# Recurrence of a hybrid layer: the transposed 32x32 inverse from VectorE block transposes instead of a third TensorE product per level

## The chip, the cores and the metric

One core of a Trainium2 chip runs the whole layer as one program. The metric is the device time of that program in microseconds (us), as the median of several executions. A profile is one execution of its own, with its own time.

## The reference

The layer takes x (1024 tokens by 1024 channels, float32) through an adaLN-modulated hybrid time mixer, a layer norm, a squared-ReLU MLP and a second layer norm. The part that matters here is the first branch of the mixer, an RWKV-7 recurrence with 8 heads of 64 channels:

```
def step(state, inp):
    r_t, w_t, k_t, v_t, a_t, b_t = inp
    sa = jnp.einsum('bhvk,bhk->bhv', state, a_t)
    state = (state * w_t[:, :, None, :] + sa[..., None] * b_t[:, :, None, :]
             + v_t[..., None] * k_t[:, :, None, :])
    return state, jnp.einsum('bhvk,bhk->bhv', state, r_t)
```

The other branch (stick-breaking attention), the merge by gates, the output projection and the MLP are not touched.

## The kernel before

The program is a row of stages: `phase_start` (adaLN, input projection), `phase_recurrence` (L809), `phase_stick`, `phase_merge`, `phase_out`, `phase_mlp`. Only `phase_recurrence` and a table of constants are changed. In the profile that stage's repeated part runs from 260 us to about 630 us.

The recurrence is computed in chunks of 64 tokens. A turn handles 2 heads (one half of the partitions each) and half of the tokens, which is 8 chunks, so there are 8 turns for 4 pairs of heads and 2 halves. Within a chunk the step by step update becomes a triangular solve: with N the strictly triangular 64x64 matrix of products between writes and reads, the kernel needs T = (1 - N)^-1. It builds T for the 32x32 diagonal blocks (8 blocks in the free direction times 4 quadrants of partitions, so 32 blocks at a time), starting with the 2x2 blocks and doubling the size four times: at each level T grows by T (level mask of N) T. The last step, from 32 to 64, is done apart with the products L1589 and L1597.

Both T (`Ts`) and its transpose (`TTs`) are kept, since TensorE takes one operand transposed. One level k = 0 to 3 before the change is:

- `correction` on TensorE (L1487): X = N T, 32 small products, which the profile shows as 64 matmul records of 32x32 since float32 products run as two records each. They write the bank `rw_invx`.
- `correction` on VectorE (L1232): takes X out of PSUM and multiplies it by the mask of the level.
- `corrected` on TensorE: T X into `rw_invx` (L1495, 64 records) and its transpose into `rw_inv` (L1498, 64 records), which accumulates over the levels.
- `inverse` on VectorE (L1228): adds the new part to `Ts`. `inverse` on ScalarE (L953): copies `rw_inv` to `TTs`.

Before level 0, `tt0` (mask times N, L1245, plus the identity, L1247) is put into both banks by products with the identity (L1530: 8 records, L1533: 64 records), and copied from there (L1224, L953).

Each engine's order is written out by hand in its own `turn(t)`; the engines meet by semaphores (`wait`), and a waiting instruction holds up all that is behind it on its engine. Five things are interleaved in a turn: the inverse for turn t; the front (decays, keys, norms) of turn n = t+1; the chain of 8 states of turn l = t-1 (L1380 on TensorE, L1169 on VectorE, each needing the other); the group norm of turns ll = t-2 (L1401, L1430) and lll = t-3 (L1360 spread, L1199 `normalised`, L1205 `gained`, L1212 `added`, L1423 `gate`). So group-norm work exists only from turn 3 on. On VectorE, `cumulate` (L1096) starts the front of the next turn, and then POOL runs L878, L882, L885, L887, L891. The reads of keys (L1236) take a whole 128x512 result out of PSUM with a mask.

PSUM has 8 banks, all taken: `BA`, `BB` (`rw_main`), `BC` (`rw_inv`), `BD` (`rw_invx`), `F` (`rw_front`), `TL` (`rw_tail`), `HY0`, `HY1` (`rw_state`). The logits of the decay (L1340) and of the rate (L1346) both go through `F`, one after the other.

Of the kernel before, what the change touches and what calls it, by code (L numbers as in the profile page):

```python
# [9 lines left out]
ALU = mybir.AluOpType  # L10
# [3 lines left out]
P = 128  # L14
# [31 lines left out]
CT = {n: i for i, n in enumerate(("ident", "causal", "small", "small2", "bones", "cent", "ahead", "misc"))}  # L46


def constants():
# [6 lines left out]
    lower = lambda s: (row // (2 * s) == col // (2 * s)) & (row % (2 * s) >= s) & (col % (2 * s) < s)  # L56
    t[:, CT["small"]] = np.select([which == 0, which == 1, which == 2, which == 3],
                                  [(row // 2 == col // 2) & (row < col), lower(2), lower(4), lower(8)])
    t[:, CT["small2"]] = np.select([which == 0, which == 1], [lower(16), row == col], 0)
# [8 lines left out]
    t[:, CT["misc"], 5] = i[:, 0] % CH < CH // 2  # L68
    reset = np.ones((P, HALF), np.float32)
# [739 lines left out]
def phase_recurrence(nc, g, a):  # L809

    with ExitStack() as es:
# [16 lines left out]
        NTs, tt0 = sb("NTs", (P, NB, 2 * B)), sb("tt0", (P, NB, B))  # L828
# [6 lines left out]
        per_turn = {"pp": 2, "M1e": 2, "NTe": 2, "M2e": 2, "ze": 2, "ge": 2, "ysb": 2, "PQ": 2, "TTe": 5, "Te": 5, "X": 4, "Xe": 4, "TX": 4,  # L835
                    "ch": NC, "S": NC}
        names = ("wa gs th kkr sq lw sg la a cum cumE eN eE eI t k2 aN ss ssm rn bc w1 AT RT BT KT wc rk BhT KhT M0 pp TT0 M1e NTe init TTe Te "
# [74 lines left out]
        def _(act):  # L912
# [19 lines left out]
            def learning_rate(n):  # L932
                if not inside(n):
                    return
                wait(act, n - 1, "k2")
                wait(act, n - 1, "aN")
                wait(act, n, "la")
                act.activation(av[:], F[:], ACT.Sigmoid, bias=col(n, A0)).then_inc(s["a"], 1)
# [20 lines left out]
            def state_maps(l):  # L959
                if not inside(l):  # L960
                    return
                wait(act, l, "ZG")
                for c2 in (1, 0):
                    if c2 == 0:
                        wait(act, l, "ze", 1)
                    act.activation(gt[:, c2::2, :], q4(BCD[c2])[:, :, HD:P], ACT.Copy).then_inc(s["ge"], 1)
# [39 lines left out]
            def turn(t):  # L1006
                f, n, l, ll, lll = t % 2, t + 1, t - 1, t - 2, t - 3
                wait(act, t, "M0")
                for e in (1, 0):
                    if e == 0:  # L1010
                        wait(act, t, "pp", 1)
                    act.activation(flat(NTs[:, 4 * e:4 * e + 4, :]), BAB[e][:, 0:2 * P], ACT.Copy).then_inc(s["NTe"], 1)
                state_maps(l)
                deviation(lll)
                inverse(t, 0)
                decay_rate(n)
                keys(n)
                inverse(t, 1)
                learning_rate(n)
                inverse(t, 2)  # L1020
                decays(n)
                inverse(t, 3)
                natural(t, "vn", flat(vn[:]), BA[:])
                natural(t, "kn", flat(kn[:]), BB[:])
                high(lll)
                inverse(t, 4)
                wait(act, t, "TTe")
                act.activation(T64[:, :, 0:B], TTs[:], ACT.Copy, scale=g.misc(5)).then_inc(s["TTm"], 1)
                natural(t, "bn", W[f][:, :, 1, :].rearrange("p (e j) n -> p j e n", e=2), q4(BA).rearrange("p j (e n) -> p j e n", e=2))
                natural(t, "an", rhs[:, :, 0:HD].rearrange("p (e j) n -> p j e n", e=2), q4(BB).rearrange("p j (e n) -> p j e n", e=2))  # L1030
                centred(ll)
                wait(act, t, "T12")
                act.activation(T64[:, :, B:CH], BC[:, 0:2 * P].rearrange("p (b n) -> p b n", n=B), ACT.Copy).then_inc(s["T12e"], 1)
                wait(act, t, "mv")
                act.activation(rhs[:, :, HD:P], BA[:].rearrange("p (b n) -> p b n", n=HD), ACT.Copy).then_inc(s["mve"], 1)
                squared(ll)
                answers(l)
# [44 lines left out]
        def _(dve):  # L1082
            small = lambda x: g.tile("small")[:, x * B:(x + 1) * B]
            over = lambda m, k: m.unsqueeze(1).to_broadcast([P, k, m.shape[-1]])
            sum32 = lambda x: g.tile("small2")[:, x * B:(x + 1) * B]
            m16, eye = sum32(0), sum32(1)
            levels = (small(1), small(2), small(3), m16)
# [84 lines left out]
            def queries(l):  # L1172
# [3 lines left out]
                for c2 in range(2):  # L1176
                    if c2:
                        wait(dve, l, "ge", 1)
                    dve.tensor_tensor(c8(zt)[:, c2::2, :], q4(BCD[c2])[:, :, 0:HD], ar[l % 2][:, 1, :].rearrange("p (c n) -> p c n", n=CH)[:, c2::2, :],
                                      ALU.add).then_inc(s["ze"], 1)  # L1180
# [40 lines left out]
            def inverse(t, k):  # L1221
                if k == 0:
                    wait(dve, t, "init")
                    dve.tensor_copy(flat(Ts[:]), BD[:, 2 * P:4 * P]).then_inc(s["Te"], 1)  # L1224
                else:
                    wait(dve, t, "TX", k)
                    wait(dve, t, "Te", k)
                    dve.tensor_tensor(flat(Ts[:]), BD[:, 2 * P:4 * P], flat(Ts[:]), ALU.add).then_inc(s["Te"], 1)  # L1228

            def correction(t, k):  # L1230
                wait(dve, t, "X", k + 1)
                dve.tensor_tensor(X[:], BD[:, 0:2 * P].rearrange("p (b n) -> p b n", n=B), over(levels[k], NB), ALU.mult).then_inc(s["Xe"], 1)  # L1232
# [6 lines left out]
            def turn(t):  # L1239
                f, n, l, ll, lll = t % 2, t + 1, t - 1, t - 2, t - 3  # L1240
                wait(dve, t, "M0")
                for e in range(2):
                    if e:
                        wait(dve, t, "NTe", 1)
                    dve.tensor_tensor(tt0[:, 4 * e:4 * e + 4, :], half4(BAB[e], 0)[:, :, 0:B], over(small(0), NT), ALU.mult).then_inc(s["pp"], 1)  # L1245
                wait(dve, t, "pp")
                dve.tensor_tensor(tt0[:], tt0[:], over(eye, NB), ALU.add).then_inc(s["TT0"], 1)  # L1247
                queries(l)
# [6 lines left out]
                write_hats(t)  # L1255
                correction(t, 0)
                reads_of_keys(t, 0)
                reads_of_keys(t, 1)
                inverse(t, 1)
                state(l, 0)  # L1260
                key_hats(t)
                correction(t, 1)
                state(l, 1)
                cumulate(n)
                inverse(t, 2)
                state(l, 2)
                normalised(lll)
                correction(t, 2)
                state(l, 3)
                gained(lll)  # L1270
                added(lll)
                inverse(t, 3)
                state(l, 4)
                gated(lll)
                correction(t, 3)
                state(l, 5)
                keys(n)
                inverse(t, 4)
# [6 lines left out]
                writes(n)  # L1285
                ends(n)
# [13 lines left out]
            queries(end)  # L1300
# [26 lines left out]
        def _(pe):  # L1327
            ident, bones = g.tile("ident"), g.tile("bones")
            eye = lambda rows: g.tile("small2")[rows, B:2 * B]
# [5 lines left out]
            def decay_logits(n):  # L1335
# [3 lines left out]
                wait(pe, n - 1, "AT")  # L1339
                pe.matmul(F[:], wa_s[0:LORA_W, n // 2 * P:(n // 2 + 1) * P], th[0:LORA_W, tok(n)], start=True, stop=True).then_inc(s["lw"], 1)  # L1340

            def rate_logits(n):
                if not inside(n):
                    return
                wait(pe, n, "sg")
                pe.matmul(F[:], wa_s[LORA_W:P, n // 2 * P:(n // 2 + 1) * P], th[LORA_W:P, tok(n)], start=True, stop=True).then_inc(s["la"], 1)  # L1346
# [967 lines left out]
```

## Time and profile before

| what | value |
| --- | --- |
| median of 3 executions | 2004.65 us (2004.02 to 2005.7) |
| the profiled execution | 2001.76 us, its span 2000.0 us |
| PE matmul busy | 1767.2 us (88%), 18163 records |
| PE weight load busy | 946.4 us, 18298 |
| DVE (VectorE) busy | 778.6 us, 1057 |
| ACT (ScalarE) busy | 569.0 us, 871 |
| POOL busy | 460.2 us, 241 |

The engines are named as in the profile: PE is TensorE (PEld its weight loads), DVE is VectorE, ACT is ScalarE. A duration of a matmul record contains its way through the array, and neighbours overlap, so the time that a group of products takes is read from the start of the group to the start of the next. Idle time with the releaser "issue" is time in which an engine waited for nothing that the profile shows. The granted clock of TensorE has two levels, written 1.00 (2.4 GHz) and 0.50 (1.2 GHz), and a number in between is a mean over a stretch.

### The profile page before, as it was taken

The page shows a single profiled execution, that of the slowest core. Times are in us where ns is not written, and L with a number is a line of the kernel's source. Part 1 is how long each engine was busy: PE and PEld are TensorE (multiplying, and loading weights), DVE is VectorE, ACT ScalarE, POOL GpSimd, SP SyncE. Part 2 cuts the span into 40 slices and gives each one's busy share as a digit, 9 for nine tenths or more (in the row PEclk, how much of TensorE's full clock was granted, in tenths as well). Part 3 has the DMA queues.
Part 4 walks back from the last instruction along what each step waited for, and adds up shares of the span by engine and source line. Part 5 has one row for each costly group of instructions (what it writes and reads, how often), then busy time and mean ns, then how long its engine had stood idle before and what let it go on. Part 6 is the DMA issues. An engine that isn't in the chain of part 4 may idle for free. (4 is left out here: it accounts for less than half of the span.)

```text
span 2000.0 us, 41125 instructions
## 1 busy us (share of the span) xinstructions
PE 1767.2 (88%) x18163; PEld 946.4 (47%) x18298; DVE 778.6 (39%) x1057; ACT 569.0 (28%) x871; POOL 460.2 (23%) x241
## 2 busy tenths in 40 slices
PE   2699778888878999988999978779999999999995
PEld 2344356666665445554444434334444444444442
DVE  7766443344442145561010148732312223122238
ACT  4111133343322135561211134433131221312202
POOL 1221021111112101111222221335251322513213
PEclk7799967787988999999999989889999999999998
DMA  9334100000010112001212221022111211212002
GB/s 332 116 126 136 52 3 4 4 4 4 4 47 23 36 50 54 1 1 43 63 34 60 105 85 32 21 95 85 53 56 40 72 31 52 67 37 85 1 1 84
DMA packets 105491, 109.93 MB, mean 55 GB/s; under 512 B 2428, under 2 KB 82442, under 8 KB 105098
## 3 DMA queue, kind: packets, MB, share of 16 engines
q1 hardware_dynamic: 105352, 107.82, 16.6%
q8 instruction: 119, 1.95, 0.4%
q14 instruction: 20, 0.16, 0.0%
HBM read 101.52 MB, written 4.19 MB: 53 GB/s over the span
## 5 line engine op out<-in xcount | busy, mean ns | idle before, releaser
L207 PE MATMUL tokens_ps<-a_hi,z 128*128 128x512 bf16 x944 | 246.9, 380 | 6.9 <-POOL z L2032 6.1
L520 PE MATMUL ff_ps<-ff_hi,c_lo 128*128 128x512 bf16 x504 | 191.0, 379 | 0.6
L520 PE MATMUL ff_ps<-ff_hi,c_hi 128*128 128x512 bf16 x500 | 189.5, 379 | 1.3 <-DVE z L2210 0.9
L520 PE MATMUL ff_ps<-ff_lo,c_hi 128*128 128x512 bf16 x500 | 189.5, 379 | 0.6
L2210 DVE TENSOR_TENSOR z<-ff_ps,z 128x512 f32<-128x512 f32 x128 | 88.3, 690 | 205.7 <-PE ff_ps L520 205.0
L2103 ACT ACTIVATE ff_r<-tokens_ps,cols 128x1024 f32<-128x1024 f32 x32 | 35.6, 1112 | 418.9 <-PE tokens_ps L207 409.2
L2032 POOL TENSOR_TENSOR z<-z 128x1024 bf16<-128x1024 f32 x30 | 70.1, 2335 | 363.7 <-ACT z L2028 363.7
L207 PEld LDWEIGHTS tokens_ps<-a_hi,z 128*128 128x128 bf16 x960 | 94.2, 98 | 120.7 <-POOL z L2032 7.1
L207 PE MATMUL tokens_ps<-a_lo,z 128*128 128x512 bf16 x469 | 141.1, 380 | 0.6
L2196 DVE TENSOR_TENSOR ff_r<-ff_r 128x1024 f32<-128x1024 f32 x32 | 44.8, 1401 | 230.1 <-ACT ff_r L2103 230.1
L1739 DVE TENSOR_TENSOR mg_ga<-mg_ga,mg_ps 128x1024 f32<-128x1024 f32 x8 | 9.8, 1221 | 202.9 <-PE mg_ps L207 202.9
L184 POOL TENSOR_TENSOR mg_wlo<-mg_stage,mg_whi 128x1024 bf16<-128x1024 f32 x21 | 44.7, 2128 | 172.1 <-ACT mg_whi L180 172.1
L207 PE MATMUL mg_ps<-a_hi,mg_whi 128*128 128x512 bf16 x248 | 75.5, 384 | 6.1 <-POOLq L78 5.7
L520 PEld LDWEIGHTS ff_ps<-ff_hi,c_hi 128*128 128x128 bf16 x512 | 50.1, 98 | 61.6 <-issue 1.3
L520 PEld LDWEIGHTS ff_ps<-ff_hi,c_lo 128*128 128x128 bf16 x512 | 50.1, 98 | 60.5
L520 PEld LDWEIGHTS ff_ps<-ff_lo,c_hi 128*128 128x128 bf16 x512 | 50.1, 98 | 60.3
L207 PE MATMUL mg_ps<-a_hi,mg_wlo 128*128 128x512 bf16 x256 | 77.1, 383 | 0.0
L2142 POOL TENSOR_TENSOR c_lo<-ff_r,c_hi 128x1024 bf16<-128x1024 f32 x32 | 68.0, 2125 | 36.7 <-ACT c_hi L2107 36.7
L207 PE MATMUL mg_ps<-a_lo,mg_whi 128*128 128x512 bf16 x248 | 75.3, 383 | 0.4
L650 DVE TENSOR_TENSOR_SCAN b_lo<-z,sb_ahead 128x256 f32<-128x256 f32 (+3 forms) x32 | 55.9, 1788 | 49.2 <-ACT z L751 49.2
L207 PEld LDWEIGHTS tokens_ps<-a_lo,z 128*128 128x128 bf16 x480 | 47.1, 98 | 56.9 <-issue 0.6
L207 PE MATMUL zs_ps<-a_hi,zs_whi 128*128 128x512 bf16 x210 | 64.3, 383 | 9.0 <-POOL zs_wlo L184 8.1
(333 smaller groups left out, 3282.0 us busy)
## 6 DMA issues: line engine op xcount, KB each, us to landing
ada_w<-w_ada SPq DMA_DIRECT2D x9, 2048.0 KB, 7.9
z<-w_ff SPq DMA_DIRECT2D x32, 512.0 KB, 4.0
ff_st<-w_ff SPq DMA_DIRECT2D x8, 2048.0 KB, 7.7
mg_stage<-w_in SPq DMA_DIRECT2D x16, 512.0 KB, 3.8
zs_stage<-w_in SPq DMA_DIRECT2D x14, 512.0 KB, 5.2
z<-w_ada SPq DMA_DIRECT2D x3, 2048.0 KB, 15.8
z<-w_in SPq DMA_DIRECT2D x8, 512.0 KB, 4.5
z<-w_out SPq DMA_DIRECT2D x1, 4096.0 KB, 14.9
```

Of the source, the lines that this page charges most:

```text
L184: pool.tensor_tensor(lo[u][:], stage[u][:], hi[u][:], ALU.subtract).then_inc(lo_ready[u], 1)
L207: last = pe.matmul(out[:, h * HALF:(h + 1) * HALF], w[:, kt, :], a[:, slot, h * HALF:(h + 1) * HALF], start=(x == 0 and y == 0), stop=(x = ...
L520: last = pe.matmul(out, a[:, slot, at], w[:, x, n], start=(x == 0 and y == 0), stop=(x == k - 1 and y == 2))
L650: dve.tensor_tensor_scan(prod[b][:, 0:nk][:, ::-1], m, masked, 1.0, ALU.mult, ALU.max).then_inc(s_scan, 1)
L1739: dve.tensor_tensor(ga[:], ga[:], ps[2][:], ALU.mult).then_inc(s_pa, 1)
L2032: pool.tensor_tensor(ff.lo[u], stage[u], ff.hi[u], ALU.subtract).then_inc(ff.lo_ready[u], 1)
L2103: act.activation(r[u][:], ps1[u][:], ACT.Relu, bias=g.cols[:, ds(gr * GT + (b1 + t), 1)]).then_inc(s_relu[u], 1)
L2142: pool.tensor_tensor(g.c_lo[:, GT * par + t, :], r[u][:], g.c_hi[:, GT * par + t, :], ALU.subtract).then_inc(s_ulo[u], 1)
L2196: dve.tensor_tensor(r[u][:], r[u][:], r[u][:], ALU.mult).then_inc(s_sq[u], 1)
L2210: dve.tensor_tensor(acc, ps2[x % 4][:], acc, ALU.add).then_inc(s_acc, 1)
```

## The change

The third product per level and the products with the identity go. `Ts` and `TTs` are related by a VectorE transpose of 32x32 blocks: `TTs` is now the first one built (mask times N plus identity) and `Ts` is its transpose; after each level, `Ts` gets its addition and is transposed into `TTs`. The four level masks are applied once per turn, to N (`NTm`, two VectorE instructions of 128x512 out), so the copy of X needs no mask and moves to ScalarE. The last level's lower part of `T64` is written by three instructions instead of one. Since the bank `rw_inv` is free during the levels, the rate logits go there and both logits products are issued together, behind `correction(t, 0)`. The orders on all engines are rearranged: `normalised` goes ahead of the second `inverse`, `gained` and `added` go between `cumulate` and `state(l, 3)`, `high` goes behind `squared`.

```
-                  [(row // 2 == col // 2) & (row < col), lower(2), lower(4), lower(8)])
-    t[:, CT["small2"]] = np.select([which == 0, which == 1], [lower(16), row == col], 0)
+    upper = lambda s: (row // (2 * s) == col // (2 * s)) & (row % (2 * s) < s) & (col % (2 * s) >= s)
+    t[:, CT["small"]] = np.select([which == 0, which == 1], [upper(1), row == col], 0)
+    t[:, CT["levels"]] = np.select([which == k for k in range(4)], [upper(2 << k) for k in range(4)])
...
 ScalarE
-            def inverse(t, k):
-                wait(act, t, *(("TX", k) if k else ("init",)))
-                act.activation(flat(TTs[:]), BC[:, 0:2 * P], ACT.Copy).then_inc(s["TTe"], 1)
+            def correction(t, k):
+                wait(act, t, "X", k + 1)
+                act.activation(flat(X[:]), BD[:, 0:2 * P], ACT.Copy).then_inc(s["Xe"], 1)
...
 VectorE
             def inverse(t, k):
...
+                wait(dve, t, "TX", k + 1)
+                wait(dve, t, "Te", k + 1)
+                dve.tensor_tensor(flat(Ts[:]), BD[:, 2 * P:4 * P], flat(Ts[:]), ALU.add).then_inc(s["Te"], 1)
+                wait(dve, t, "Te", k + 2)
+                dve.transpose(flat(TTs[:]), flat(Ts[:])).then_inc(s["TTe"], 1)
...
+                dve.tensor_tensor(TTs[:], TTs[:], over(eye, NB), ALU.add).then_inc(s["TT0"], 1)
+                wait(dve, t, "TT0")
+                dve.transpose(flat(Ts[:]), flat(TTs[:])).then_inc(s["Te"], 1)
+                queries(l, 1)
                 wait(dve, t, "NTe")
+                for e in range(2):
+                    dve.tensor_tensor(NTm[:, 4 * e:4 * e + 4, :, :], half4(BAB[e], 0)[:, :, 0:B].unsqueeze(2).to_broadcast([P, NT, 4, B]), levels,
+                                      ALU.mult).then_inc(s["NTm"], 1)
+                queries(l, 0)
...
+                write_hats(t)
                 inverse(t, 0)
                 reads_of_keys(t, 0)
                 reads_of_keys(t, 1)
                 state(l, 0)
                 key_hats(t)
                 state(l, 1)
+                normalised(lll)
+                inverse(t, 1)
+                state(l, 2)
                 cumulate(n)
                 gained(lll)
                 added(lll)
+                state(l, 3)
+                inverse(t, 2)
+                gated(lll)
+                state(l, 4)
+                keys(n)
+                state(l, 5)
                 inverse(t, 3)
...
 TensorE
             def corrected(t, k):
-                wait(pe, t, "TTe", k + 1)
                 wait(pe, t, "Xe", k + 1)
+                if k:
+                    wait(pe, t, "TTe", k)
                 for e, j, b in blocks:
                     for q in quads:
-                        pe.matmul(BD[q, (NB + b) * B:(NB + b + 1) * B], TTs[q, b, :], X[q, b, :], start=True, stop=True)
-                for e, j, b in blocks:
-                    for q in quads:
-                        last = pe.matmul(BC[q, b * B:(b + 1) * B], X[q, b, :], TTs[q, b, :], start=False, stop=True, skip_group_check=True)
+                        last = pe.matmul(BD[q, (NB + b) * B:(NB + b + 1) * B], TTs[q, b, :], X[q, b, :], start=True, stop=True)
                 last.then_inc(s["TX"], 1)
...
-                for q in quads:
-                    pe.matmul(BC[q, 0:2 * P], eye(q), flat(tt0[q, :, :]), start=True, stop=True)
-                for e, j, b in blocks:
-                    for q in quads:
-                        last = pe.matmul(BD[q, (NB + b) * B:(NB + b + 1) * B], tt0[q, b, :], eye(q), start=True, stop=True)
-                last.then_inc(s["init"], 1)
                 answer_terms(l)
...
                 correction(t, 0)
+                logits(n)
+
+                corrected(t, 0)
...
                 chain(l, 0)
+
+                correction(t, 1)
                 deviations(lll)
                 chain(l, 1)
                 corrected(t, 1)
                 wait(pe, t, "M2e")
                 natural(t, "vn", zs(8, t), BA)
+                chain(l, 2)
+
+                correction(t, 2)
+                gate(lll)
+                chain(l, 3)
+
+                corrected(t, 2)
                 wait(pe, t, "KhT")
                 natural(t, "kn", kh, BB)
                 chain(l, 4)
+
+                correction(t, 3)
```

## Rows read from the trace of the kernel before

**Rows 1.** Stretches of one turn each (from:to, length, busy and instructions by engine, clock, DMA share, GB/s).

```profile
260.30:301.30 41.00, 31.59 (x1140) 25.63 (x1140) 13.67 (x29) 13.72 (x24) 6.25 (x5) 0.66 0.02 4
301.30:343.70 42.40, 36.24 (x1364) 30.08 (x1364) 16.40 (x40) 15.15 (x28) 6.25 (x5) 0.76 0.02 4
343.70:389.00 45.30, 39.91 (x1376) 31.30 (x1376) 16.96 (x41) 16.03 (x30) 6.26 (x5) 0.77 0.02 4
389.00:436.50 47.50, 41.44 (x1399) 31.63 (x1399) 20.04 (x46) 18.20 (x33) 7.35 (x6) 0.82 0.02 4
436.50:486.60 50.10, 43.52 (x1398) 33.77 (x1397) 21.14 (x46) 18.39 (x33) 7.55 (x6) 0.76 0.02 4
486.60:530.50 43.90, 37.38 (x1395) 29.07 (x1394) 20.93 (x46) 18.11 (x33) 7.55 (x6) 0.92 0.02 4
530.50:575.00 44.50, 36.32 (x1399) 28.14 (x1398) 20.95 (x46) 18.00 (x33) 7.54 (x6) 0.96 0.12 43
575.00:630.00 55.00, 39.44 (x1527) 32.33 (x1526) 16.01 (x41) 16.32 (x35) 8.95 (x9) 0.84 0.03 11
```

**Rows 2.** Order of time on PE in the turn from 486.6 us, single groups.

```profile
490.79 0.63 PE L1530 MATMUL rw_inv<-rec_tt,const 32*32 32x256 f32 x8
...
491.90 0.58 PE L1466 MATMUL rw_state<-c_lo,rec_vn 64*64 64x64 f32 x24
...
505.75 0.71 PE L1498 MATMUL rw_inv<-rec_TT,rec_X 32*32 32x32 f32 x62
506.38 0.33 PE L1380 MATMUL rw_state<-rec_st,rec_gt 64*64 64x64 f32 x4
507.86 1.10 PE L1423 MATMUL rw_tail<-z,rec_g_s 128*128 128x512 f32 x2 [1.14 <-DVE rec_yc L1199]
508.88 0.75 PE L1487 MATMUL rw_invx<-rec_T,rec_NTs 32*32 32x32 f32 x64
...
510.32 0.60 PE L1478 MATMUL rw_main<-const,rec_kh 128*128 128x128 f32 x4
```

**Rows 3.** Groups by line, 260 to 630 us (count, busy us, mean ns, idle before).

```profile
L1498 PE MATMUL rw_inv<-rec_TT,rec_X 32*32 32x32 f32 x2048 | 30.9, 206 | 16.1 <-issue 15.8
L1487 PE MATMUL rw_invx<-rec_T,rec_NTs 32*32 32x32 f32 x2048 | 30.3, 211 | 11.9 <-issue 9.8 <-DVE rec_T L1228 1.8
...
L1466 PE MATMUL rw_state<-c_lo,rec_vn 64*64 64x64 f32 x256 | 7.0, 226 | 7.0 <-issue 7.0
...
L1423 PE MATMUL rw_tail<-z,rec_g_s 128*128 128x512 f32 x10 | 6.4, 728 | 5.7 <-DVE rec_yc L1199 5.7
...
L1224 DVE COPY rec_T<-rw_invx 128x256 f32<-128x256 f32 x8 | 3.4, 424 | 7.0 <-PE rw_invx L1533 6.7
```

**Rows 4.** DMA queues, 486.6 to 530.5 us (packets, MB, share of the 16 engines).

```profile
q8 instruction: 11, 0.18, 1.7%
```

**Rows 5.** Order of time on DVE in the turn from 486.6 us, single instructions.

```profile
499.23 1.29 DVE L1236 TENSOR_TENSOR c_lo<-rw_main,const 128x512 f32<-128x512 f32 x2 [2.05 <-PE rw_main L1547]
...
504.50 1.22 DVE L1096 TENSOR_TENSOR_SCAN rec_cum<-reset,rec_sg 128x512 f32<-128x512 f32 x1
...
510.02 0.27 DVE L1169 SCALAR_TENSOR_TENSOR rec_st<-rec_st,rec_wc,rw_state 128x64 f32<-128x64 f32 x1
510.21 1.48 DVE L1205 TENSOR_SCALAR rec_yc<-rec_yc,cols 128x512 f32<-128x512 f32 x1
511.73 1.64 DVE L1212 TENSOR_TENSOR rec_yc<-rec_yc,rec_rk 128x512 f32<-128x512 f32 x1
...
517.04 0.54 DVE L1103 TENSOR_SCALAR rec_k<-rec_av,cols 128x512 f32<-128x512 f32 x1
```

**Rows 6.** Order of time on POOL in the same turn.

```profile
510.13 1.27 POOL L885 TENSOR_TENSOR rec_sg<-rec_kkr,rec_sg 128x512 f32<-128x512 f32 x1
511.36 1.45 POOL L887 TENSOR_TENSOR rec_ar<-z,rec_cum 128x512 f32<-128x512 f32 x1
```

**Rows 7.** A stretch with a long "issue" gap on PE (columns as in the first group).

```profile
466.50:467.80 1.30, 0.04 (x5) 0.00 (x0) 0.00 (x0) 0.21 (x1) 0.00 (x0) 1.00 0.00 0
...
468.90:482.40 13.50, 12.88 (x272) 9.63 (x272) 4.59 (x12) 4.15 (x8) 2.37 (x2) 0.50 0.02 4
```

More of the change, by code:

```diff
@@ L43 @@
 PAIR_ROWS = ("w0", "a0", "kk", "ka", "rk", "gng", "gnb")
-CT = {n: i for i, n in enumerate(("ident", "causal", "small", "small2", "bones", "cent", "ahead", "misc"))}
+CT = {n: i for i, n in enumerate(("ident", "causal", "small", "levels", "bones", "cent", "ahead", "misc"))}
 def constants():
@@ L962, in state_maps @@
                 wait(act, l, "ZG")
-                for c2 in (1, 0):
-                    if c2 == 0:
+                for c2 in range(2):
+                    if c2:
                         wait(act, l, "ze", 1)
@@ L1036, in turn @@
                 squared(ll)
+                high(lll)
                 answers(l)
@@ L1084, in _ @@
             over = lambda m, k: m.unsqueeze(1).to_broadcast([P, k, m.shape[-1]])
-            sum32 = lambda x: g.tile("small2")[:, x * B:(x + 1) * B]
-            m16, eye = sum32(0), sum32(1)
-            levels = (small(1), small(2), small(3), m16)
+            eye = small(1)
+            levels = g.const[:, CT["levels"], :].rearrange("p (k n) -> p k n", n=B).unsqueeze(1).to_broadcast([P, NT, 4, B])
             strict, incl = (g.tile("causal")[:, x * CH:(x + 1) * CH] for x in range(2))
@@ L1175, in queries @@
                 wait(dve, l, "ZG")
[L1176 to L1180, printed above, removed]
+                if c2 == 0:
+                    wait(dve, l, "ge", 1)
+                dve.tensor_tensor(c8(zt)[:, c2::2, :], q4(BCD[c2])[:, :, 0:HD], ar[l % 2][:, 1, :].rearrange("p (c n) -> p c n", n=CH)[:, c2::2, :],
+                                  ALU.add).then_inc(s["ze"], 1)
             def bonus(l):
@@ L1241, in turn @@
                 wait(dve, t, "M0")
+                wait(dve, l, "TTm")
                 for e in range(2):
@@ L1285, in turn @@
                 writes(n)
+                wait(dve, t, "T12")
+                wait(dve, t, "TTm")
+                dve.tensor_copy(T64[CH:CH + B, :, B:CH], BC[CH:CH + B, 0:2 * P].rearrange("p (b n) -> p b n", n=B)).then_inc(s["T12e"], 1)
                 ends(n)
@@ L1299, in _ @@
             end = TURNS - 1
-            queries(end)
+            queries(end, 1)
+            queries(end, 0)
             state0(end)
@@ L1333, in _, with logits @@
             blocks = [(e, j, 4 * e + j) for j in range(NT) for e in range(2)]
-            def decay_logits(n):
+            def logits(n):
                 if not inside(n):
@@ L1339, in decay_logits @@
                 wait(pe, n - 1, "AT")
+                wait(pe, n - 2, "ze")
+                wait(pe, n - 2, "ge")
                 pe.matmul(F[:], wa_s[0:LORA_W, n // 2 * P:(n // 2 + 1) * P], th[0:LORA_W, tok(n)], start=True, stop=True).then_inc(s["lw"], 1)
[L1342 to L1346, printed above, removed]
+                pe.matmul(BC[:], wa_s[LORA_W:P, n // 2 * P:(n // 2 + 1) * P], th[LORA_W:P, tok(n)], start=True, stop=True).then_inc(s["la"], 1)
             def squares(n):
@@ L1351, in squares @@
                 wait(pe, n, "sq")
-                wait(pe, n, "a")
+                wait(pe, n, "sg")
                 for j in range(NT):
@@ L1582, in turn @@
                 natural(t, "bn", bh, BA)
+                chain(l, 5)
+                corrected(t, 3)
+                bonus(ll)
                 wait(pe, t, "kne")
                 natural(t, "an", ar[f][:, 0, :], BB)
+                chain(l, 6)
                 wait(pe, t, "Te")
@@ L1588, in turn @@
                     for q in (0, 2):
-                        last = pe.matmul(BD[quads[q + 1], b * B:(b + 1) * B], NTs[quads[q], b, B:2 * B], Ts[quads[q], b, :], start=True, stop=True)
+                        last = pe.matmul(BD[quads[q + 1], b * B:(b + 1) * B], NTx[quads[q], b, :], Ts[quads[q], b, :], start=True, stop=True)
                 last.then_inc(s["X21"], 1)
@@ L1594, in turn @@
                 wait(pe, t, "TTe")
+                if inside(n):
+                    wait(pe, n, "a")
                 for e, j, b in blocks:
@@ L1618, in _ @@
             pe.wait_ge(s["th"], 2)
-            decay_logits(0)
-            rate_logits(0)
+            logits(0)
             squares(0)
```

95 lines of the change are left out of this document (25 added, 70 removed).

## The prediction, as put on record before the changed kernel was run

> **What bounds the kernel now.** Only the recurrence stage is touched, so I read that stage alone, first in stretches of one turn [rows 1]. A turn takes 41.0 to 50.1 us (the last stretch also holds the start of the tail). PE has products in flight for 31.6 to 43.5 us of it, DVE for 14 to 21, ACT for 14 to 18, POOL for 6 to 9. Such a busy share proves little, so the second view is the order of time on PE in one turn [rows 2]: group follows group, each starting a fraction of a microsecond after the one before, and the only real wait on another engine in a full turn is the one ahead of the gate product (1.14 us, until L1199 on DVE is done; 5.7 us over the 5 turns that have it [rows 3]). The dependence T, X, T X, T is hidden, since the order puts a chain step, a spread or a projection between each product and the next that needs it. PE's own instruction stream is the bound.
>
> The third view, the groups by line [rows 3], adds what the stream suffers from: idle time ended by "issue", 15.8 us ahead of records of L1498, 9.8 ahead of L1487, 7.0 ahead of L1466. The DMA queues say what this is [rows 4]: 11 packets of instructions, 0.18 MB, in one turn, so 16 KB each. A turn has 1395 matmul and 1394 weight-load records [rows 1]; 2789 over 11 is about 254 instructions a packet. PE runs dry where small records are issued faster than packets arrive.
>
> **The removed products.** L1498: 2048 records, 30.9 us busy in 32 groups [rows 3]; the last record of a group (about 0.19 us, nearly its mean of 206 ns) overlaps the next group, so 30.9 - 32 x 0.19 = 24.8 us of stream, mixed over both clocks (at the full clock a group takes 506.38 - 505.75 = 0.63 us [rows 2]). The products with the identity run from 490.79 to 491.90 [rows 2]: 1.11 x 8 = 8.9 us. Together **33.7 us**.
>
> What such a record costs is where a rule and the trace part. The row gives 0.63 us for 62 records, 10 ns each, since four quadrants run beside one another. The Trainium skill, TensorEngine Tiling (Array Packing), section Instruction Overhead, says that each matmul carries about 60 cycles of overhead however short it is; at 2.4 GHz that is 25 ns, and the 328 records removed per turn would be 8.2 us a turn, an estimate of 66 us in all. I take the row; the same page lets tiles overlap, and the trace shows it.
>
> **The "issue" gaps.** The bound above is that all 15.8 us ahead of L1498 go; the bound below is that they only move to the next dense group. A turn sheds 328 of 1395 records, 24%, and so 24% of the packets. 24% of 15.8 + 9.8 + 7.0 is 7.7 us. The neighbours that now meet (L1487 with a projection, L1495 with transposes) are less dense than L1495 with L1498. I take **10 us**, and keep 0 and 16.
>
> **The wait at the gate.** `normalised` moves ahead of the second `inverse`, and the gate product behind the third `correction`. The 5.7 us [rows 3] go: **5.7 us**.
>
> **What DVE gets.** Five transposes of 128x256 a turn, which the trace doesn't show. Nearest is the copy of the same shape, L1224, 0.42 us [rows 3]; below that I put nothing, above it a stretched instruction: L1205 took 1.48 us while POOL ran L885 and L887 [rows 5, 6], and the same form took 0.54 us with POOL idle (L1103 [rows 5]), a factor of 2.7, so 0.42 to 1.1 us. I take 0.42, 2.1 us a turn. The two `NTm` instructions read PSUM and write 128x512 each as the two of L1236 do: 1.29 us [rows 5]. One small copy for `T64` adds 0.4. What goes: four masked copies of X and the first copy of T, 5 x 0.42 = 2.1 us (ACT takes the copies of X in place of its own of `TTs`). Net +1.7 us on an engine busy 21 of 44 us: free, unless it falls on a step that PE waits for. There are two such steps.
>
> First, the head of a turn. `correction(t, 0)` needs `NTm`. From the end of M0, DVE does two masks (0.7), the identity (0.4), a transpose (0.4), one query (0.4) and `NTm` (1.3), 3.2 us by the prices above. PE has queries, state terms and answer terms in between, about 2.9 us without the 2 us of gaps that mostly fall there. I charge 0.2 us a turn: **-1.5 us**, and keep 0 to 8.
>
> Second, the middle. Between the second `inverse` and `state(l, 3)` DVE now has a transpose 0.42, a state 0.27, `cumulate` 1.22, `gained` 1.48, `added` 1.64 and the state 0.27 [rows 5]: 5.3 us. PE has in that time `correction` 0.63, the gate 508.88 - 507.86 = 1.02, a chain step 0.3, `corrected` 0.6 (as many small records) and a transposed tile 0.5 (its 0.60 less the overlap) [rows 2], 3.0 us, and then stands at chain(4), with `correction(t, 3)` behind it. So 2.3 us of new wait in the 5 turns with group norm: **-11.5 us**. It would be near 0 if POOL's work fell elsewhere, and 20 if transposes stretch too.
>
> **What I cost at nothing.** The paired logits are the same two products; their sigmoids come one after the other on ACT. The X copies on ACT (I price them as L1224, 0.42 us) are covered by the projection, spread, gate or squares that follow each `correction`; uncovered, each would show about 0.5 us, 32 times. The only one near its cover is the fourth, behind the exponentials of `decays`. The extra copies into `T64` end before PQ, behind two product groups and the norm spread (3 us). `high` moves to ACT's slack near the turn's end; POOL's low part follows in time for the next turn. No DMA is added, and SP's queue is untouched.
>
> **Sum.** 33.7 + 10 + 5.7 - 11.5 - 1.5 = 36.4 us. The profiled execution took 2001.76 us and would become 1965.4; the median of the runs lies 2.9 above it, so 1968.3, and I say **1968 us**.
>
> **Rivals.**
> 1. *The gaps go with L1498 and the middle wait is hidden* by them: 33.7 + 15.8 + 5.7 - 2 = 53 us, 1952. For it: the gaps are the larger part of what separates a turn from its bare stream. Against it: the head's dense part stays.
> 2. *DVE becomes the bound in the middle*: transposes at 1.1 us in the window in which POOL works, two to three of them per turn on the path, 2 us x 8 = 16 less: 1984. For it: the stretched L1205 and L1212. Against it: a transpose has one source, and only L1212, with two, and L1205 are seen stretched.
> 3. *The clock falls, and the result is slower.* PE stood still from 466.5 to 467.8 us at clock 1.00 and was then granted 0.50 for 13.5 us [rows 7]. With fewer records and a new wait of 2.3 us in the middle, such stretches could spread. The price: two turns with the same work took 50.1 us at 0.76 and 43.9 at 0.92 [rows 1], 0.39 us per 0.01 of mean clock. The mean over the turns is now 0.81; if all ran at the first turn's 0.66, that is 15 x 0.39 x 8 = 47 us lost against 36 won: 2015. It decides from a mean of 0.81 - 4.55/0.39/100 = 0.69 down. Against it: the long "issue" gaps, which are what stands ahead of the fall in the row, get fewer too. The Trainium skill, TensorE: Matmul & The Clock Gate, section HAM oscillation, warns of bursts with pauses between, and speaks against this change; by that rule the trace agrees, since the fall follows a pause.
> 4. *The stream was not what the turn's length came from*, and the shorter stream only waits elsewhere: within 4 us of 2004.65. Against it: a single wait on another engine in a full turn.
>
> **Chances.** Forecast (1956 to 1980) 0.62; rival 1 0.13; rival 2 (1980 to 2000) 0.13; rival 4 0.04; rival 3 0.08. The range takes in the forecast, most of rivals 1 and 2, and the bounds of the gaps (10 less, 6 more) and of the new waits (8 more, 9 less): 1946 to 1990. A measurement of this kernel tells 0.2%, 4 us, from no change. Faster 0.88, same 0.04, slower 0.08.
>
> **What would show it.** Right: a full turn has about 1067 matmul records and some 8 instruction packets; turns of 38 to 44 us; the first `state` after `added` ends a PE wait of about 2 us in turns 3 to 7; no wait ahead of the gate; transposes near 0.42 us; mean clock 0.76 to 0.86. The stages before and after unchanged. Wrong: PE waiting for `Xe` or `TTe` at several levels (the dependence is exposed after all), transposes of 1 us or more, a clock under 0.7, or turns shortened by less than 3 us with gaps merely moved to L1487 and L1495.

## The result, and the profile after

The median went from 2005.18 us (the kernel before, run again beside it) to 1916.34 us (1915.55 to 1919.04), a ratio of 0.955 with an interval of 0.952 to 0.958: 84 to 96 us less, where 36 had been forecast and 1946 was the lower end of the range. The direction was right, the size was not. The profiled execution has a span of 1914.1 us.

All of it lies in the recurrence. The first product of the value projection behind the turns (L1654, now L1638) starts at 546.4 us instead of 633.5, and the stages after it keep their lengths. The stretches of one turn of the changed kernel, with the columns of [rows 1]:

```profile
258.40:291.30 32.90, 25.67 (x812) 21.05 (x812) 16.74 (x32) 13.55 (x24) 6.85 (x5) 0.65 0.01 3
291.30:326.80 35.50, 28.48 (x1036) 23.93 (x1037) 18.94 (x43) 14.86 (x28) 6.94 (x5) 0.86 0.02 4
326.80:362.40 35.60, 31.05 (x1048) 24.89 (x1048) 19.87 (x44) 15.84 (x30) 6.84 (x5) 0.86 0.02 5
362.40:396.40 34.00, 29.61 (x1067) 23.59 (x1067) 23.48 (x49) 17.90 (x33) 7.81 (x6) 1.00 0.02 4
396.40:431.10 34.70, 31.04 (x1071) 24.50 (x1070) 23.15 (x49) 17.87 (x33) 7.82 (x6) 0.95 0.02 4
431.10:467.90 36.80, 31.36 (x1069) 24.61 (x1068) 22.95 (x49) 18.02 (x33) 7.82 (x6) 0.95 0.02 4
467.90:501.50 33.60, 29.73 (x1070) 23.75 (x1069) 22.99 (x49) 17.99 (x33) 7.82 (x6) 1.00 0.12 38
501.50:547.00 45.50, 32.63 (x1217) 26.57 (x1218) 18.19 (x45) 16.15 (x35) 10.11 (x9) 0.93 0.11 36
```

A full turn has 1067 to 1071 matmul records, as forecast, but takes 33.6 to 36.8 us where 38 to 44 had been expected, against 43.9 to 50.1 before [rows 1]. Two views in one row each make the comparison easier: the first seven turns as one stretch, first the kernel before, then the changed one (same columns).

```profile
260.30:575.00 314.70, 266.39 (x9460) 209.62 (x9460) 130.09 (x294) 117.59 (x214) 48.76 (x39) 0.81 0.03 9
```

```profile
258.40:501.50 243.10, 206.94 (x7163) 166.32 (x7163) 148.12 (x315) 116.04 (x214) 51.89 (x39) 0.90 0.03 9
```

The seven turns take 71.6 us less for 2297 records less, 31 ns each. The time per record hardly moved (314.7 / 9460 = 33.3 ns, 243.1 / 7163 = 33.9 ns). The mean granted clock went from 0.81 to 0.90. The time in which PE had nothing in flight fell from 48.3 to 36.2 us, and the rest, 59 us, came out of "busy", which holds the time in which records ran at the lower clock.

The groups by line of the changed kernel, 258 to 547 us, answer [rows 3]:

```profile
L1493 PE MATMUL rw_invx<-rec_X,rec_TT 32*32 32x32 f32 x2048 | 29.9, 206 | 12.0 <-issue 10.0 <-ACT rec_X L953 1.7
L1484 PE MATMUL rw_invx<-rec_T,rec_NTm 32*32 32x32 f32 x2048 | 28.3, 201 | 14.9 <-issue 11.9 <-DVE rec_NTm L1247 2.9
...
L1225 DVE STREAM_TRANSPOSE rec_TT<-rec_T 128x256 f32<-128x256 f32 x32 | 14.2, 445 | 1.1
L1223 DVE TENSOR_TENSOR rec_T<-rw_invx,rec_T 128x256 f32<-128x256 f32 x32 | 13.5, 423 | 45.8 <-PE rw_invx L1493 45.6
...
L1247 DVE TENSOR_TENSOR rec_NTm<-rw_main,const 128x512 f32<-128x512 f32 x16 | 10.2, 673 | 0.0
...
L1418 PE MATMUL rw_tail<-z,rec_g_s 128*128 128x512 f32 x10 | 5.9, 655 | 1.0 <-issue 1.0
```

A transpose takes 445 ns (0.42 us had been taken), `NTm` 673 ns, the wait ahead of the gate is gone, and the wait for `NTm` at the head of a turn is 2.9 us in all (1.5 charged). The dependence is still covered: matmuls wait 1.7 us in all for the copies of X on ACT.

The middle of a turn, where a new wait of 2.3 us had been charged, in order of time, first on DVE, then the POOL instruction that falls into it, then on PE:

```profile
483.10 1.22 DVE L1096 TENSOR_TENSOR_SCAN rec_cum<-reset,rec_sg 128x512 f32<-128x512 f32 x1
484.23 0.52 DVE L1204 TENSOR_SCALAR rec_yc<-rec_yc,cols 128x512 f32<-128x512 f32 x1
484.78 1.64 DVE L1211 TENSOR_TENSOR rec_yc<-rec_yc,rec_rk 128x512 f32<-128x512 f32 x1
486.34 0.27 DVE L1169 SCALAR_TENSOR_TENSOR rec_st<-rec_st,rec_wc,rw_state 128x64 f32<-128x64 f32 x1
```

```profile
484.39 1.48 POOL L878 TENSOR_TENSOR rec_sg<-rec_cum,rec_sg 128x512 f32<-128x512 f32 x1 [18.38 <-DVE rec_cum L1096]
```

```profile
474.13 0.66 PE L1340 MATMUL rw_front<-z,rec_wa_s 64*128 64x512 f32 x1
474.14 0.69 PE L1341 MATMUL rw_inv<-z,rec_wa_s 64*128 64x512 f32 x1
...
485.74 0.66 PE L1473 MATMUL rw_main<-const,rec_kh 128*128 128x128 f32 x4
486.67 0.50 PE L1375 MATMUL rw_state<-rec_st,rec_gt 64*64 64x64 f32 x4 [0.27 <-DVE rec_st L1169]
```

`gained` took 0.52 us: it started 0.16 us before POOL's L878, while `added` (L1211) started inside L878 and took 1.64 us. The chain step waited 0.27 us, and all chain steps of the stage together waited 1.4 us. The stretching has moved rather than gone: L1105, behind the place where `gained` had been, took 692 ns before and takes 1638 ns now. The rows also show what I had missed: the two logits products, each with 64 rows, start 0.01 us apart and run side by side.

### The profile page after: what moved, and what is told of

The parts are those of the page before. It is cut to its first block and busy times, and to the rows that moved or that the text cites. A ratio compares the mean times of both kernels' runs of the same rounds, so it can differ in the third digit from the quotient of the medians.

```text
span 1914.1 us, 35930 instructions
## 1 busy us (share of the span) xinstructions
PE 1696.1 (89%) x15539; PEld 894.7 (47%) x15674; DVE 798.6 (42%) x1081; ACT 566.9 (30%) x871; POOL 463.8 (24%) x241
## 5 line engine op out<-in xcount | busy, mean ns | idle before, releaser
L184 POOL TENSOR_TENSOR mg_wlo<-mg_stage,mg_whi 128x1024 bf16<-128x1024 f32 x21 | 44.6, 2125 | 170.9 <-ACT mg_whi L180 170.9
L520 PEld LDWEIGHTS ff_ps<-ff_hi,c_hi 128*128 128x128 bf16 x512 | 50.1, 98 | 61.7 <-issue 1.3
L520 PEld LDWEIGHTS ff_ps<-ff_hi,c_lo 128*128 128x128 bf16 x512 | 50.1, 98 | 60.4
L520 PEld LDWEIGHTS ff_ps<-ff_lo,c_hi 128*128 128x128 bf16 x512 | 50.1, 98 | 60.3
```

The source lines that it names most:

```text
L184: pool.tensor_tensor(lo[u][:], stage[u][:], hi[u][:], ALU.subtract).then_inc(lo_ready[u], 1)
L520: last = pe.matmul(out, a[:, slot, at], w[:, x, n], start=(x == 0 and y == 0), stop=(x == k - 1 and y == 2))
```

## The experiments

All times are medians beside the kernel before, run side by side, whose own time varied from 2006.6 to 2013.5 us from one comparison to the next; the ratios are to be compared. The changed kernel stands at 0.955, and at 0.957 (0.954 to 0.960) when it was run again (e14), so a difference of 5 us between two comparisons can't be told from none. Traces have a spread of their own: the trace of the kernel before is of an execution of 2001.76 us, while its executions beside e1 took 2002 to 2022 us.

**e1, the kernel before without the third product.**

```
-                for e, j, b in blocks:
-                    for q in quads:
-                        last = pe.matmul(BC[q, b * B:(b + 1) * B], X[q, b, :], TTs[q, b, :], ...)
```

> The kernel before, with the third product of each level (L1498, the transposed part) left out, so TTs stays at its first value and the output is not the reference's; all waits and orders stay. Theory A (the removed records at their own price): 24.8 us of stream and 8 to 16 us of issue gaps go, 33 to 41 us less than before, mean clock of the turns stays near 0.81. Theory B (the shorter stream also brings the clock up, which I had not counted): 45 to 60 us less, mean clock of the turns 0.88 or more. Theory C (the gaps only move): 20 to 27 us less.

1947.28 us, ratio 0.966 (0.963 to 0.970): 67 us less than before by the ratio. Nothing else was changed, so 2048 records are worth 60 to 75 us, 29 to 37 ns each, about three times the 12 ns of stream at which I had them. Theories A and C fall on the size; B, with 45 to 60 us, comes nearest. The first seven turns:

```profile
260.70:528.60 267.90, 236.72 (x7667) 185.55 (x7668) 127.83 (x294) 116.92 (x214) 48.69 (x39) 0.83 0.03 10
```

The clock is 0.83 in this trace, little above 0.81. The two traces differ by 46.8 us in these turns and by 54.4 us in their spans, less than the 67 us of the medians. Over the whole program the four executions of e1 had a mean clock of 0.943, and the kernel before, beside them, 0.929, so that a part of the 67 us may be the clock; how large a part, this run doesn't tell.

**e2, the changed kernel with T X issued twice.**

```
+                for e, j, b in blocks:
+                    for q in quads:
+                        pe.matmul(BD[q, (NB + b) * B:(NB + b + 1) * B], TTs[q, b, :], X[q, b, :], start=True, stop=True)
```

> The changed kernel with the product T X of each level issued twice into the same place (256 more records per turn, about as many as the change removed, same output). Theory A (records at their own price): 8 x 2.6 = 21 us plus 8 to 16 us of issue gaps, 29 to 37 us slower than the changed kernel, clock unchanged near 0.92. Theory B (density drives the clock as well): 45 us or more slower, clock back to about 0.82. If most of the gain came from the new orders instead, it stays under 30 us.

1978.13 us, 0.982 (0.978 to 0.986), 54 us by the ratios (62 by the medians) above the changed kernel: 26 to 30 ns for each of 2048 records put back. The clock of the seven turns is 0.83, where B said 0.82. So a record costs about the same in both directions, and in the new order as in the old, with what the clock does included: it fell from 0.90.

**e3, the logits apart.**

```
                 logits(n)
                 corrected(t, 0)
+                rate_logits(n)
```

> The changed kernel with the rate logits issued behind corrected(t, 0), 64 small records after the decay logits, instead of right behind them. Theory P (the two logits products use different halves of the rows of the array and run at the same time when issued together): 7 turns x 1.0 us, and up to 2.0 at the lower clock, 7 to 12 us slower than the changed kernel. My prediction's view (the same two products wherever they stand): within 2 us.

1915.96 us, 0.951 (0.948 to 0.955): no slower than the changed kernel. The products do run side by side in the trace of the changed kernel, and yet apart they cost nothing that shows. The profiled execution, 1927.4 us, was the slowest of its five; the other four lie within 1.5 us. Its seven turns hold the records of the changed kernel, at a clock of 0.86:

```profile
259.20:512.30 253.10, 221.55 (x7164) 172.93 (x7164) 149.03 (x315) 116.31 (x214) 51.56 (x39) 0.86 0.03 8
```

**e4, `normalised` and the gate in their old places.**

```
-                normalised(lll)
                 inverse(t, 1)
                 state(l, 2)
+                normalised(lll)
...
+                gate(lll)
                 correction(t, 2)
-                gate(lll)
```

> The changed kernel with normalised back behind the second inverse and state(l, 2) on VectorE, and the gate product back ahead of correction(t, 2) on TensorE, as in the kernel before. Prediction's term: the wait ahead of the gate returns, 1.1 us in each of 5 turns, 5 to 8 us slower than the changed kernel. Rival (the wait was swallowed by issue gaps that come anyway): within 2 us.

1928.63 us, 0.958 (0.955 to 0.962). The wait is back in its full size (5.4 us, 5.7 before), and the seven turns, with the same number of records again, took less time at a higher clock than those of e3:

```profile
L1418 PE MATMUL rw_tail<-z,rec_g_s 128*128 128x512 f32 x10 | 6.0, 682 | 5.4 <-DVE rec_yc L1198 5.4
```

```profile
259.10:501.50 242.40, 203.96 (x7164) 164.11 (x7164) 148.62 (x315) 115.18 (x214) 53.04 (x39) 0.91 0.03 9
```

The price of the wait in time, 6 us by the ratios against the first run of the changed kernel and 3 against the second, agrees with the term of 5.7, but the intervals overlap: not settled.

The seven turns of e3 and e4 give a price of the clock. Six traces (the changed kernel twice, e3, e4, e7, e8) have 7160 to 7164 records in the seven turns; the shortest of them is e4 and the longest e3, 10.7 us apart for 0.05 of clock, 2.1 us per 0.01. The prediction's own price, 0.39 us per 0.01 and turn, is 2.7 us for seven turns. Both are estimates from two stretches each.

**e5, the third product of the kernel before as one large product.**

```
-                for e, j, b in blocks:
-                    for q in quads:
-                        last = pe.matmul(BC[q, b * B:(b + 1) * B], X[q, b, :], TTs[q, b, :], ...)
+                last = pe.matmul(BC[:, 2 * P:4 * P], ident, rk[t % 4][:, 0:2 * P], start=True, stop=True, ...)
```

> The kernel before, with the 64 small records of each third product replaced by one product of 128x128 with 256 columns (2 records) into the unused half of the same bank: about the same time on the array (half of the 1.02 us of a 512-column product, 0.5 us, against 0.63), but 62 records fewer. TTs is then wrong, and so is the output. Theory S (what counts is the time on the array): at most 10 us less than before. Theory F (what counts is the number of instructions to be brought in: 2 packets of 256 instructions a turn less at 3.5 us each): 40 to 58 us less, nearly as much as with the product left out (58 us).

1949.76 us, 0.971 (0.969 to 0.973), 58 us less than before (54 to 62). The array's work is nearly kept (L1496 up to 540 us), and the second row shows the seven turns:

```profile
L1496 PE MATMUL rw_inv<-rec_rk,const 128*128 128x256 f32 x56 | 21.5, 468 | 0.0
```

```profile
260.40:530.50 270.10, 240.54 (x7720) 182.74 (x7720) 128.55 (x294) 117.09 (x214) 48.66 (x39) 0.91 0.03 10
```

21.5 us in the 28 groups up to there against the 24.8 that I took for 32 groups of L1498, and no gap ahead of them. Still most of what leaving it out brought is there (58 of 67 us, from two comparisons with intervals of 54 to 62 and 60 to 75). So the gain hangs on the number of small records, each with its weight load, and not on their time on the array: Theory S falls as it stood, and F has the size. Records and weight loads were not tried apart.

The run doesn't settle by which way fewer records save time, because the clock rose too, from 0.81 to 0.91. Of the 44.6 us that these turns lost, 18.7 are time with nothing in flight (48.3 before, 29.6 now). At 2.1 to 2.7 us per 0.01 the clock is worth 20 to 26 us, an estimate. Together that is 39 to 45 us, nearly all of it. Array time, gaps and a rising clock, added up, fit this run as well as Theory F does.

**e6, the kernel before without the products with the identity.**

```
-                for q in quads:
-                    pe.matmul(BC[q, 0:2 * P], eye(q), flat(tt0[q, :, :]), start=True, stop=True)
-                for e, j, b in blocks: ...
-                    dve.tensor_copy(flat(Ts[:]), BD[:, 2 * P:4 * P]).then_inc(s["Te"], 1)
+                    dve.tensor_copy(flat(Ts[:]), flat(tt0[:])).then_inc(s["Te"], 1)
```

> The kernel before, without the products with the identity that set up T and its transpose (72 records a turn); both copies take tt0 instead, so T starts transposed and the output is wrong. My prediction's price: 8.9 us less than before plus 2 of gaps. Theory F: 72 of 128 records a packet, 0.56 packets x 3.5 us x 8 turns = 16 us less, more if the clock comes up too.

1983.02 us, 0.989 (0.987 to 0.992), 22 us less (17 to 26) for 576 records: 29 to 45 ns each. The prediction's 8.9 plus 2 is half of it, and here the clock can't explain it: the mean over the program is 0.931 with and without these products, and the seven turns had 0.81 in both traces. The packets of instructions in the seven turns go with the records; here those of the kernel before, then of the changed one (packets, MB):

```profile
q8 instruction: 74, 1.21, 1.6%
```

```profile
q8 instruction: 56, 0.92, 1.6%
```

74 and 56 packets in 314.7 and 243.1 us are one in 4.3 us in both. It isn't a fixed rhythm: the same 56 packets took 253.1 us in e3, one in 4.5 us, and e5 needed 60 in 270.1 us, also one in 4.5.

**e7, `gained` and `added` later.**

```
                 cumulate(n)
-                gained(lll)
-                added(lll)
                 state(l, 3)
                 inverse(t, 2)
+                gained(lll)
+                added(lll)
```

> The changed kernel with gained and added on VectorE moved behind state(l, 3) and the third inverse. My prediction's middle wait (2.3 us in 5 turns) would go: 8 to 11 us faster than the changed kernel. What the trace of the changed kernel shows (about 0.4 us a turn at that place): within 2 us.

1923.97 us, 0.960 (0.957 to 0.962): no gain; whether some us are lost, against 0.955 and 0.957, is not settled. There was no wait of 2.3 us to remove.

**e8, every transpose into TTs twice.**

```
+                dve.transpose(flat(TTs[:]), flat(Ts[:])).then_inc(s["TTd"], 1)
+                wait(dve, t, "TTd", k + 1)
                 dve.transpose(flat(TTs[:]), flat(Ts[:])).then_inc(s["TTe"], 1)
```

> The changed kernel with each of the four transposes of a turn into TTs done twice (1.8 us more on VectorE per turn). Rival 2 of the prediction (VectorE at its bound in the middle of a turn): 8 us slower or more. VectorE with slack: within 3 us of the changed kernel.

1916.93 us, 0.955 (0.953 to 0.957), the changed kernel's own time. DVE was busy 10.1 us longer in the seven turns (158.2 against 148.1) and it cost nothing; rival 2 falls.

**e9, a filler product in the changed kernel.**

```
+                if k:
+                    if inside(t + 1):
+                        wait(pe, t + 1, "a")
+                    last = pe.matmul(BC[:, 2 * P:4 * P], ident, rk[t % 4][:, 0:2 * P], start=True, stop=True)
                 last.then_inc(s["TX"], 1)
```

> The changed kernel with one extra product of 128x128 with 256 columns (2 records, 0.5 us on the array at the full clock) behind T X at each of the last three levels, its result unused. Theory S (time on the array): 3 x 0.5 x 8 = 12 us slower than the changed kernel, more at the lower clock. Theory F (instructions; an issue gap elsewhere shrinks by what the filler takes): 6 records a turn, 0 to 4 us slower.

1911.51 us, 0.952 (0.949 to 0.955): with 12 us of extra work it is no slower; the 5 us by which the median is lower lie within the intervals. The first seven turns:

```profile
259.30:497.20 237.90, 203.23 (x7206) 163.03 (x7206) 147.62 (x315) 115.41 (x214) 51.84 (x39) 0.97 0.03 9
```

The clock is 0.97 where the changed kernel had 0.90.

**e10, spreads as transposes of an expanded vector.**

```
-                    for e in range(2):
-                        last = pe.matmul(dst[heads[e], j * P:(j + 1) * P], small[:, ...].to_broadcast([P, HD]), ident, ...)
+                    last = pe.transpose(dst[:, j * P:(j + 1) * P], small[:, j * P:(j + 1) * P], ident)
...
+                dve.tensor_copy(c8(tmp), rn[:].unsqueeze(2).to_broadcast([P, NB, HD])).then_inc(s["rn"], 1)
```

> A version meant to be faster: the two spreads of a turn (norms and deviations) are 4 transposes each (4 records) of a vector that VectorE has copied out to 128x512 into a buffer free at the time, instead of 8 products (16 records). 24 records a turn less on TensorE, about 0.9 us a turn more on VectorE. Theory F at 30 ns a record: 5 to 6 us faster than the changed kernel, and with the 0.5 us of array time per spread up to 12. If the VectorE copies land on a step that TensorE waits for: no faster, or a few us slower.

1910.5 us, 0.951 (0.949 to 0.954), by the ratios 8 us under the first run of the changed kernel, with intervals that overlap, and 11 under the second.

**e11, the new orders undone with T X twice.** The edits of e2, e3 and e4 together.

> The changed kernel with T X issued twice, the logits apart and normalised and the gate in their old places, together (256 of the 328 removed records are back). If the parts add up: 62 + 0 + 5, 67 us slower than the changed kernel, 1975 to 1992 us. If the new orders matter only when the stream is short: about 62 us or less.

1990.88 us, 0.991 (0.988 to 0.994): 73 us by the ratios above the changed kernel, where the parts give 54 + 0 + 6 = 60. With the 22 us of e6 on top that is 95 us, against the 90 of the whole change. The parts add to within what the intervals of some 6 us each allow; the clock of the seven turns was down to 0.79.

**e12, e10 and e9 together; e13, the filler in the kernel before (there it also disturbs the transpose accumulated in the same bank); e14, the changed kernel again.**

```
+                if k:
+                    last = pe.matmul(BC[:, 2 * P:4 * P], ident, rk[t % 4][:, 0:2 * P], start=True, stop=True, ...)
```

> The changed kernel with both the expanded spreads (5.8 us faster in the earlier run) and the filler product behind T X at the last three levels (4.8 us faster in the earlier run, though it adds 12 us of array time). If the filler works by holding the clock up and the spreads by leaving instructions out, they add: 8 to 12 us faster than the changed kernel in the same call. If both only shortened the same issue gaps: 5 to 6 us.

> The kernel before with the same filler product behind the third product of the last three levels (3 x 0.5 us a turn on the array, 6 records more), result unused. Theory clock: the mean clock of the turns rises from 0.81 to 0.88 or more and pays for the filler and more, 0 to 15 us faster than before. Theory time on the array: 12 us or more slower. Theory gaps alone (no effect on the clock): 0 to 5 us slower.

> The changed kernel itself, run beside the two others on the same chip, so that differences of a few us can be read: 1912 to 1922 us; and a second profile of it, which shows how far the clock of single turns differs between executions (turn for turn within 0.15, the mean of the turns within 0.03).

e12: 1911.45 us, 0.951 (0.949 to 0.954). e14: 1922.17 us, 0.957 (0.954 to 0.960). e12 is 11 us faster than e14 side by side, as forecast if the two add; against e9 (0.952) and e10 (0.951), which ran in another comparison, it adds nothing. Whether they add is not settled. e13: 2021.25 us, 1.005 (1.002 to 1.007), 4 to 14 us slower. The seven turns of e12, e13 and e14:

```profile
260.00:495.00 235.00, 201.97 (x7073) 161.93 (x7073) 152.05 (x326) 115.61 (x214) 51.22 (x39) 0.94 0.03 8
```

```profile
259.50:598.60 339.10, 283.55 (x9499) 216.40 (x9500) 128.43 (x294) 117.37 (x214) 48.32 (x39) 0.80 0.03 9
```

```profile
259.40:503.00 243.60, 208.51 (x7163) 167.72 (x7164) 149.54 (x315) 115.68 (x214) 51.43 (x39) 0.89 0.03 9
```

In the changed kernel the filler goes with a higher clock and costs nothing; in the kernel before the clock stays (0.80) and the filler costs 4 to 14 us, about its 12 us of array time, though it adds only 48 records (1.4 us at 30 ns each). So the number of records isn't the whole price either: array time counts where the clock doesn't make up for it.

## Why the prediction was wrong

**The removed products and the gaps: the step that failed.** "I take the row", 10 ns a record, gave 33.7 us, and 10 more for the gaps, 43.7 in all for 2624 records, at a clock that was to stay where it was. Undone one by one in the kernel before they are worth 67 (e1, 60 to 75) and 22 us (e6, 17 to 26), 89 together: 34 ns a record. That alone is the whole result of 90. The row was right as a pitch (0.63 us for 62 records) and wrong as a price. e5 shows that the price hangs on the number of small records: 2 records with nearly the array time of 64 save almost all of it. The gaps themselves did what I said: PE's time with nothing in flight fell by 12.1 us. The other part sat inside "busy", of which 59 us went where 29.5 (seven eighths of 33.7) were expected.

**Where the missing 30 us of "busy" went.** The sum had no term for a rising clock; the clock stood in it only as a rival, and as a loss. It rose by 0.09, and at 2.1 to 2.7 us per 0.01 that is 19 to 24 us, an estimate. So most of the missing part of these turns may be the clock, and it counts among what the removed records bring, since the clock rose when they went. It isn't all: e6 brought twice its price with the clock unchanged. What part is the clock and what part is short pauses under records in flight, no run divides.

**The page against the row.** The Trainium skill, TensorEngine Tiling (Array Packing), section Instruction Overhead, had given 25 ns per matmul and 66 us for this change, and I set it aside. Its figure came much nearer the measured 26 to 37 ns per record (e1, e2). But these runs do not show its reason at work: packed groups do start every 10 ns [rows 2], and the measured price contains the gaps and the clock.

**What the supply is.** Each packet is 16 KB, and its count goes with the records (74 to 56). That the long "issue" gaps are waits for packets can be read from the times of the packets in the traces. In the changed kernel packets start at 473.61, 477.34 and 480.73 us, and these two rows are the first records after a gap:

```profile
476.24 0.64 PE L1493 MATMUL rw_invx<-rec_X,rec_TT 32*32 32x32 f32 x50 [0.73 <-issue]
...
479.60 0.39 PE L1484 MATMUL rw_invx<-rec_T,rec_NTm 32*32 32x32 f32 x24 [1.05 <-issue]
```

They start 2.6 and 2.3 us after a packet's start. In the seven turns all 28 such gaps over 0.3 us end 2.2 to 3.0 us after one (all 32 of the kernel before 2.2 to 2.8), and no two packets start less than 3.3 us apart in either trace. At that distance a record with its weight load has 26 ns, the size of the measured price. But the middle distance is 3.9 us, so the supply is at its limit in dense stretches only, and the time with nothing in flight holds only 12.1 of the 71.6 us. The Trainium skill, Advanced Engine Details and Errata, section ISA Cache, says that instructions are kept in lines of 16 KB, 256 instructions each. The packet size in the trace agrees.

**The clock.** I expected 0.76 to 0.86 and had only its fall as a rival. It was 0.90 and 0.89. That it matters is seen in e9, where 12 us of added work came with 0.97 and no loss, and in e3 and e4. The kernel before shows it by itself: of its 17 executions beside e14 the fastest took 1997.17 us at a mean clock of 0.941 over the program, the slowest 2017.85 us at 0.924. It isn't the whole cause: e6 won 22 us with no change of it. Why it rose is open. Rival 3, slower by a falling clock, didn't come.

**The gate**, 5.7 us: gone from the trace, back with e4; its price in time lies between 3 and 6 us, unsettled. **The middle wait**, -11.5 us: the second step that failed, 0.27 us in the turn shown and 1.4 us in the stage. I had priced `gained` at the 1.48 us that it took beside L885 and L887; ahead of POOL's work it took 0.52. e7 and e8 both say that DVE has slack there. **The head wait**, -1.5: 2.9 us, mis-sized by little. **The logits**, costed at nothing: the reason was wrong (they overlap when paired), the price right (e3). **Rival 1** (1952 us) had the sign of my error, but it counted only visible gaps too, and held the clock. What each part of the change brings: leaving out the third product 67 us, leaving out the products with the identity 22; for the orders nothing certain is left, and only the gate, with 3 to 6 us, has a run of its own.

## What to carry to other kernels

Where TensorE runs many tiny products, count instructions, not only time on the array. Here a small record was worth 26 to 45 ns when it was left out or put back (e1, e2, e6), whatever its own pitch of 10 ns. The test is cheap: replace a group of small products by one large product of the same array time, and see whether the gain of leaving the group out is there. Read the granted clock of both traces beside it, and price it from two stretches with the same records: where it moved, the run tells that the records count, but not by which way. Work that another engine can do in one instruction (a block transpose, one mask over all levels) was here worth far more than the busy time that it takes from TensorE.

## What the runs showed that I had not expected

- 64 small records replaced by 2 with nearly the same array time: 58 us of the 67 that leaving them out brings, with the clock of the seven turns at 0.91 where it had been 0.81.
- Two products with 64 rows each, on different halves of the rows and in different banks, start 0.01 us apart and end together (L1340, L1341), 1.06 us for both; yet issuing them apart cost nothing in this stream.
- A filler of 12 us of array work made the changed kernel no slower (1911.51 us) with the clock at 0.97, while the same filler cost the kernel before 4 to 14 us with the clock at 0.80. Why the clock answers in one and not in the other is open.
- The same TENSOR_SCALAR of 128x512 on DVE took 1.48 us beside two POOL instructions [rows 5, 6] and 0.52 us where it started 0.16 us ahead of one; the TENSOR_TENSOR L1211 behind it, which started inside that POOL instruction, was still stretched to 1.64 us.
- Every long "issue" gap of PE in the seven turns ends 2.2 to 3.0 us after the start of a packet of instructions, and packets never start less than 3.3 us apart.
